# A shift row multiplied in native fp32 from the unsplit weights, in four column groups of the array

## The reference, cut to what matters

```
mod = c_act @ w_mod[l] + b_mod[l]
shift1, scale1, gate1, shift2, scale2, gate2 = split(mod, 6)
u = _rms(h, norm1_w[l]) * (1.0 + scale1) + shift1
proj = u @ w_in[l]                      # q, k, v, gates ... of the second block
...
u = _rms(h, norm2_w[l]) * (1.0 + scale2) + shift2
ff = silu(u @ w_gate[l]) * (u @ w_up[l])
h = h + gate2 * (ff @ w_down[l])
```

## Time and profile before

| | |
|---|---|
| median of 3 runs | 2783.16 us (2783.07 to 2783.49) |
| the profiled execution, its own time | 2784.83 us |
| its span, first to last instruction | 2783.0 us |
| PE busy | 2757.1 us (99%) |
| DVE, ACT, POOL busy | 2069.1, 1473.6, 335.8 us |
| mean granted TensorE clock | 0.998 of 2.4 GHz |
| share of the DMA engines' time | 66.7% |

### The profile page before, as it was taken

How to read it: one execution, slowest core, us unless ns; L and a number is a source line. 1 busy time by engine, 2 the same in 40 slices (tenths; PEclk the granted TensorE clock), 3 DMA queues, 4 the chain that set the end, 5 groups by cost and what they waited for, 6 DMA issues and landing times. The chain is left out here.

```text
span 2783.0 us, 43554 instructions
## 1 busy us (share of the span) xinstructions
PE 2757.1 (99%) x16354; PEld 2386.3 (86%) x16354; DVE 2069.1 (74%) x3601; ACT 1473.6 (53%) x2417; POOL 335.8 (12%) x1005
## 2 busy tenths in 40 slices
PE   7999999999999999999999999999999999999999
PEld 4778888888888888888888888888888888888888
DVE  3478877878988878787887777778888765566654
ACT  3365444545666676666667544545454443444443
POOL 0023300000002424224242310000000000000000
PEclk9999999999999999999999999999999999999999
DMA  8966668888965555555555588788768756655554
GB/s 325 352 226 212 205 204 271 286 270 294 303 177 194 175 175 174 173 181 166 182 178 172 177 278 280 258 285 296 263 209 287 247 183 188 197 189 186 189 183 148
DMA packets 183412, 621.87 MB, mean 223 GB/s; under 512 B 20241, under 2 KB 28705, under 8 KB 182433
## 3 DMA queue, kind: packets, MB, share of 16 engines
q1 hardware_dynamic: 183200, 619.09, 66.7%
HBM read 612.70 MB, written 4.21 MB: 222 GB/s over the span
## 5 line engine op out<-in xcount | busy, mean ns | idle before, releaser
L272 PE MATMUL ps<-act,whi 128*128 128x512 f32 (+1 forms) x6560 | 1763.6, 398 | 4.9 <-DVE act L257 3.0
L257 DVE TENSOR_TENSOR wlo<-raw,whi 128x1024 fp32r<-128x1024 f32 (+3 forms) x883 | 1045.3, 1189 | 437.0 <-ACT whi L248 244.1
L272 PEld LDWEIGHTS ps<-act,whi 128*128 128x128 f32 (+1 forms) x6560 | 1165.3, 189 | 217.3 <-issue 16.4
L272 PE MATMUL ps<-act,wlo 128*128 128x256 f32 (+2 forms) x6416 | 994.1, 287 | 0.4 <-DVE wlo L257 0.4
L248 ACT ACTIVATE whi<-raw 128x1024 fp32r<-128x1024 f32 (+3 forms) x883 | 880.2, 1024 | 175.8 <-PE ps L272 145.5
L272 PEld LDWEIGHTS ps<-act,wlo 128*128 128x128 f32 (+1 forms) x6416 | 896.7, 190 | 66.7 <-issue 1.7
L248 ACT ACTIVATE t<-ps 128x256 f32<-128x256 f32 (+2 forms) x420 | 157.3, 376 | 473.5 <-PE ps L272 445.6
L267 DVE SCALAR_TENSOR_TENSOR acc<-raw,c_act,acc 128x1024 f32<-128x1024 f32 x210 | 267.9, 1278 | 1.0 <-DMA raw<-in_w_mod 1.0
L248 ACT ACTIVATE t<-t 128x256 f32<-128x256 f32 (+3 forms) x258 | 114.5, 445 | 184.7 <-DVE t L257 152.0
L263 POOL TENSOR_SCALAR small<-small 128x2 f32<-128x2 f32 (+3 forms) x256 | 88.3, 345 | 972.8 <-DVE small L263 953.4
L257 POOL TENSOR_TENSOR small<-small 128x2 f32<-128x2 f32 (+2 forms) x460 | 160.0, 348 | 277.9 <-ACT t L248 187.3
(11 more groups left out here) (218 smaller groups left out, 1859.4 us busy)
## 6 DMA issues: line engine op xcount, KB each, us to landing
raw<-in_w SPq DMA_DIRECT2D x418, 512.0 KB, 4.9
raw<-in_w_mod SPq DMA_DIRECT2D x192, 512.0 KB, 4.6
raw<-in_w_gate SPq DMA_DIRECT2D x88, 512.0 KB, 4.6
raw<-in_w_up SPq DMA_DIRECT2D x88, 512.0 KB, 4.5
raw<-in_w_s SPq DMA_DIRECT2D x64, 512.0 KB, 6.8
raw<-in_w_out SPq DMA_DIRECT2D x64, 512.0 KB, 5.7
raw<-in_w_down SPq DMA_DIRECT2D x64, 448.0 KB, 3.7
raw<-in_w_ada SPq DMA_DIRECT2D x32, 512.0 KB, 5.1
```

What stands on the lines that cost most here:

```text
L257: return (q or DV).put(lambda e: e.tensor_tensor(o, a, b, op), needs, cost=max(0.4, size(o) * 0.0036) if q else 0.07 + size(o) * 0.00104)
L272: return PE.put(lambda e: e.matmul(o, w, x, start=start, stop=stop), needs, tell, cost)
```

## The change

`mm_shift` is called once per late block, ahead of the block's tile products. It multiplies the unsplit weights, straight from the `raw` slot, with the shift: four matmuls (one for each K tile of the block), 32 columns wide on the side of the shift, of which only the first is not zero, and 256 columns (two weight columns of 128) long, in native fp32. Each of the four goes to its own 32-row part of one PSUM bank. After late block 3 the bank's 256 columns are copied to SBUF by DVE, two matmuls against `C_SEL` add the four parts and turn the row into columns, and DVE copies the two sums. The shift no longer needs to be split: a tile of `t2` is filled with zeros by two ACT copies and its first column of each K tile with the shift by a third. The slot of a late piece is now free only when PE has read it too (`raw_free`).

```
--- before.py
+++ after.py
@@ -178,8 +178,6 @@
     at += 576
     SM = [place(f"small{i}", [128, 8], F32, at + 32 * i) for i in range(32)]
     at += 1024
-    SH = place("shift", [128, 16, 2], F32R, at)
-    at += 128
     T2 = [place(f"t2_{i}", [128, 512], F32, at + 2048 * i) for i in range(6)]
     T2R = [place(f"t2r_{i}", [128, 512], F32R, at + 2048 * i) for i in range(6)]
     T2R += [place(f"tx2r_{i}", [128, 512], F32R, a_c + 2048 * i) for i in range(4)]
@@ -471,7 +469,8 @@
             t = copy(hi, raw, it["in"] + (pe_free["hi", n - NH] if n >= NH else []))
             u = lo_part(lo, raw, hi, it["in"] + t + (pe_free["lo", n - NL] if n >= NL else []))
             it["hi"], it["lo"] = t, u
-            raw_free[it["raw"]] = t + u
+            if "late" not in it:
+                raw_free[it["raw"]] = t + u
         elif kind == "M":
             kt, half = it["kt"], it["half"]
             raw = RAW[it["raw"] % NR][:, 0:1024]
@@ -560,6 +559,8 @@
         hi, lo = HI[n % NH], LO[n % NL]
         last = None
         at = 0
+        if "late" in it:
+            mm_shift(it)
         for u in it["units"]:
             if it["kts"][0] == 0:
                 u.bank, free = grab_bank()
@@ -568,8 +569,6 @@
                 x, needs = ready(u.rhs, kt)
                 w = slice(at, at + 128)
                 mm_hi(u, hi[:, w], x, kt == 0, needs + it["hi"])
-                if "late" in it:
-                    mm_shift(it["late"], it["units"].index(u), kt, hi[:, w], lo[:, w], it["lo"])
                 last = mm_lo(u, lo[:, w], x, kt == 15, it["lo"], kt == it["kts"][-1])
                 at += 128
                 if kt != it["kts"][-1]:
@@ -581,27 +580,43 @@
         if "late" in it:
             for kt in it["kts"]:
                 state["used", it["late"], kt] = last
-            if kt == 15:
-                start(shift_sums(it["late"], last))
-
-    def mm_shift(name, i, kt, hi, lo, needs):
-
-        if kt == 0 and i == 0:
+
+    def mm_shift(it):
+
+
+        name, kts = it["late"], it["kts"]
+        if kts[0] == 0:
             while ("shift", name) not in state:
                 rest()
             state["sums", name], free = grab_bank()
-            PE.wait(free + state["shift", name])
-        o = state["sums", name][:, 2 * i:2 * i + 2]
-        mm(o, hi, SH[:, kt, :], kt == 0 and i == 0, False, cost=0.06)
-        mm(o, lo, SH[:, kt, :], False, kt == 15 and i == 1, needs, cost=0.06)
+            PE.wait(free + state["shift", name][1])
+        bank = state["sums", name]
+        tile = state["shift", name][0]
+        sh = tile[:, :].rearrange("p (k s) -> p k s", k=16)
+        w = RAW[it["raw"] % NR][:, :].rearrange("p (u k c) -> p u k c", u=2, k=4)
+        PE.wait(it["in"])
+        for k, kt in enumerate(kts):
+            last = mm(both(bank[32 * k:32 * k + 32, 0:256]), sh[:, kt, :], w[:, :, k, :], kt < 4, kt >= 12, tell=k == 3, cost=0.11)
+        raw_free[it["raw"]] = it["hi"] + it["lo"] + last
+        if kts[-1] == 15:
+            t2.give(tile, last)
+            start(shift_sums(name, last))
 
     def shift_sums(name, tok):
-        sm, f = yield from small.take()
-        yield from hop(tok + f)
+        rows, f = yield from t1.take()
+        sm, f2 = yield from small.take()
+        yield from hop(tok + f + f2)
         bank = state["sums", name]
-        k = copy_v(sm[:, 0:4], bank[:, 0:4], tok + f)
+        k = copy_v(rows[:, :], bank[:, 0:256], tok + f)
+        yield k
+        PE.wait(k)
+        for i in range(2):
+            t = mm(bank[:, 2 * i:2 * i + 2], rows[:, 128 * i:128 * i + 128], col(C_SEL, 2), True, True, tell=i == 1)
+        t1.give(rows, t)
+        yield from hop(t)
+        k = copy_v(sm[:, 4:6], bank[:, 0:4:2], t + f2)
         banks.give(bank, k)
-        state["offset", name] = sm, tt(sm[:, 4:6], sm[:, 0:4:2], sm[:, 1:4:2], ALU.add, k)
+        state["offset", name] = sm, k
 
     def join_late(name, i, bank, tok):
 
@@ -1184,7 +1199,7 @@
         state["halves", slot] = state.get(("halves", slot), 0) + 1
         if state["halves", slot] == 2:
             yield state["sec", slot]
-            section(slot, state["sec", slot])
+            yield from section(slot, state["sec", slot])
 
     def section(slot, needs):
 
@@ -1195,9 +1210,12 @@
         elif slot == M_MOD + 4:
             state["scale", "u2"] = stt(MOD[:, M_A2, :], MOD[:, slot, :], 1.0, col(C_N2, 16), ALU.add, ALU.mult, needs)
         elif slot in (M_MOD, M_MOD + 3):
-            h = copy(SH[:, :, 0], MOD[:, slot, :], needs + state.get(("used", "u", 15), []))
-            l = lo_part(SH[:, :, 1], MOD[:, slot, :], SH[:, :, 0], h)
-            state["shift", "u" if slot == M_MOD else "u2"] = h + l
+            tile, f = yield from t2.take()
+            yield from hop(needs + f)
+            sh = tile[:, :].rearrange("p (k s) -> p k s", k=16)
+            for i in range(2):
+                h = copy(sh[:, 8 * i:8 * i + 8, :], K1[:, 0:256].rearrange("p (k s) -> p k s", k=8), needs + f, scale=0.0)
+            state["shift", "u" if slot == M_MOD else "u2"] = tile, copy(sh[:, :, 0], MOD[:, slot, :], h)
 
     def m_items():
         secs = [(M_GATE, 0, C_BADA + 32, lambda kt, h: src["w_ada"][128 * kt:128 * kt + 128, 1024 * h:1024 + 1024 * h])]
```

## The result

The changed kernel takes 2795.41 us (median of 5 runs, 2793.02 to 2796.54), the kernel before 2783.27 (2783.07 to 2783.75). The ratio is 1.0040, 95% interval [1.0029, 1.0051]: the change makes the kernel about 12 us slower, where 2787.4 us and at most 2791 were forecast. The profiled execution took 2794.49 us.

What follows compares the result with a forecast made beforehand. PE's stream was taken as the bound, busy 2757.1 of 2783.0 us. Products -7.2, D1 stall +8.4, "u2" stalls +1.35 and clock +1.7 gave +4.2 on 2783.16: 2787.4 us, range 2778 to 2791 us.

Steps and rivals of the forecast that it cites:

- 6.9 us and half a piece: SP's queue, group "u": last constant issued at 794.5, landing at 801.9 us, between 801.3 and 802.7; ACT's slack was 2.2 us.
- PE's late blocks: Group "u": 3.55 us per late block, late block 3 from 791.8 to 795.4 us; late blocks of 16 instead of 20.
- SP's wait for PE: SP in group "u": DMA of D3's piece, ahead of S3's, waits for PE's shift product of late block 3, until 792.6 us.
- the L of K tile 4 and then of K tile 6 behind two `wlo`: DVE at D1: L 4 ready at 805.4, wanted at 801.4; L 6 at 810.0, behind the `wlo` of D2 and S2.
- products, both groups, with the selection: PE, both groups: 7.1 us go per group and 3.5 come, net 3.6 us per group, -7.2 us for both.
- stall of D1: PE in group "u": +8.4 us, 4.0 from the constants and 4.4 from two `wlo` ahead of L 6; bounds 2.0 and 9.2.
- lower clock: PE after the stalls: one stretch of 3.4 us of work at half pace loses 1.7 us; bounds 0 and 3.4.
- stalls of "u2": Group "u2": L of K tile 3 late by 1.05 us and K tile 11 by 0.3, +1.35 us; bounds 0 and 2.5.
- 0.76 us per visit: PE, late blocks: four new matmuls cost 0.76 us per visit, four visits per group, 3.0 us; bounds 0.57 and 1.1.
- Rival D: PE's late blocks: visits cost 1.1 instead of 0.76 us through changes of form, 2.7 us more; called improbable, no numeric chance.
- Rival A: Group "u": constants come in time, only DVE's order stalls D1, by 2.0 us; 2779.3 us in all; chance 0.20.
- rival C: D1: pauses leave PE at 1.2 GHz for 6.0 us of work or more; over 2788.7, up to 2791.1 us; chance 0.13.

Runs made afterwards that it cites:

- same_order: Changed kernel with only the three constant loads issued earlier on SP, planner still told the old times, so PE, ACT and DVE keep their orders: 2784.02 us.
- act_copies_late: Changed kernel, loads unmoved on SP, but the four ACT instructions behind the constants moved behind S3; the planner reordered DVE and PE too: 2781.34 us.
- held_slots: Kernel before with its own shift products, but late blocks' raw slots held until PE has done the block's first tile product: 2795.03 us.
- consts_early: Changed kernel with the three constant loads issued behind late block 0's piece, the planner told when they really come: 2778.35 us.
- early_cost19: consts_early with the planner told 0.19 instead of 0.11 us for each shift matmul: 2777.89 us, and 2777.60 us when run again.
- only_u2: The change made in group "u2" alone, group "u" as in the kernel before: 2781.82 us.
- small_first: Changed kernel with only the two 8 KB loads (ea, dtb) issued behind late block 0's piece, k staying behind the waiting pieces: 2794.58 us.

## Why the forecast was wrong

**The mechanism was right, two of its sizes were not.** Two steps failed. The last constant was to land 6.9 us and half a piece after its issue, and took 10.4 us. And the order of the second block was put at nothing, and cost 2.8 us.

PE's late blocks, SP's wait for PE, the constants behind it, ACT's queue, the L of K tile 4 and then of K tile 6 behind two `wlo`: each stands in the trace where the forecast has it, and same_order, act_copies_late and held_slots take it apart. The sign of the sum was forecast too, but not the size, and the forecast gave 0.57 to a time within 0.2% of before and only 0.28 to a slower one. Term by term, in us:

| term | forecast | measured | from |
|---|---|---|---|
| products, both groups, with the selection | -7.2 | -7.3 | twice 15.86 against 19.97 with the selection, 0.36 + 0.08 |
| stall of D1 | +8.4 | +11.0 | 7.99 + 3.02 |
| lower clock | +1.7 | +2.6 | half of 8.29 - 3.02 |
| stalls of "u2" | +1.35 | +2.2 | 1.12 + 1.07 |
| order of the second block | not there | +2.8 | 788.92 against 786.10 |
| sum | +4.2 | +11.3 | the medians differ by 12.1 |

**The products.** 0.76 us per visit and 0.4 for the selection were good to 0.1 us: late block 2 lasts 3.60 us in the trace, from 787.10 to 790.70, and eight tile products at 0.35 us leave 0.8 for the visit. Rival D, with 1.1, is out.

**The stall.** The mis-sized step is the landing of the last constant: 6.9 us and half a piece, at most 802.7 us, was taken over from a time when D3's piece stood 3.6 us ahead of S3's. Now the two were issued 0.5 us apart, right ahead of k. The forecast charged 1.35 us for a piece in the way, its bytes at the full 389 GB/s, and half of that; in the trace S3's piece took 3.1 us longer to land than before. The last packet of k came 2.8 us behind that instead of 1.7. Together with 0.2 us at the last count, and less the 0.8 us by which the last small load was issued later behind k, these are the 3.5 us between 6.9 and 10.4. The rate meanwhile was far below 389 GB/s:

```profile
795.00:803.00 8.00, 5.31 (x33) 4.42 (x31) 0.00 (x0) 0.00 (x0) 0.00 (x0) 1.00 0.93 274
```

The DMA engines were busy 93% of this stretch at 274 GB/s; no run shows why the rate was lower than in rows 12. The rest of the difference is that the group began 1.16 us earlier in this execution, so that D1 was due at 800.15 instead of 801.4. Against that, the second part was 3.0 instead of 4.4 us, because PE at half clock took longer to reach K tile 6.

Rival A's price of 2.0 us is what same_order measured, 1.7 + 0.3; its chance of 0.20 was high for a slack of 2.2 us against an issue moved by more than 5 us.

The sentence on the page "DMA: Bandwidth & Descriptors" of the Trainium skill (anatomy of one DMA), about 2.0 us and the bytes at 436 GB/s, is a fit to single DMAs issued from GpSimd. It gives an estimate of 4.0 us for k, where k's last packet ended after 7.1 us before, and after 11.2 us now. Here SyncE issued, and no transfer was alone; no run tells which of the two matters.

**The clock.** It fell while PE stood still and came back at 816.4, after 5.3 us of work at the lower pace instead of the 3.4 taken from the row near the start. That is inside the bounds, and rival C's mechanism in part; rival C had asked for 6.0 us or more. The 0.8 us by the Trainium skill ("TensorE: Matmul & The Clock Gate", the section on how the oscillation bites in real kernels) were a third of it.

**What was left out altogether.** The forecast compared the orders only around the two groups; its sum has no term for what comes later. The planner writes the rest of the program from its own clock, and that clock had moved: 13 more batches of small products and 1.6 us of small waits over the second block. same_order has them without the stall of 8 us; consts_early, early_cost19 and only_u2 (362, 361 and 361 batches, 786.0, 786.3 and 786.1 us) don't have them. With the measured sizes of the first four terms and without this one, the sum is +8.5, or 2791.7 us, 0.7 above the range, so the late landing, with the clock behind it, reaches just past the range, and this term carries the time well out of it.

**What stays open.** The reason that a batch more costs about 0.2 us (2.8 / 13) was not measured by itself; held_slots (4.3 us for 15 batches, 3.4 of them idle) shows that waits and batches come mixed. Of the 12.1 us of the medians, 0.8 are not accounted for; runs of the changed kernel differ by up to 3.5 us. (The spans of the two traces differ by only 9.7 us, of which the 1.16 us by which group "u" began earlier is a part: 11.3 - 1.16 = 10.1.)

## What to carry to other kernels

A buffer that is freed by a later reader delays everything that stands behind its refill on the issuing queue, and what is hurt may be on a third engine: look at what follows on the queue of the DMAs first, and move the transfers that wait for nothing ahead of those that do. Take the time to landing from a stretch with as many bytes issued right ahead as there will be, and price a transfer in the way by such a stretch too, not by the fullest rate. Where several loads count up one semaphore, only the last landing in the profile is to be trusted. Where a planner writes the order, compare the whole program, and tell the planner the cost that was measured.

## What the hardware showed unexpectedly

- Two matmuls of 2 columns cost 0.22 us in a stream of long ones: 0.57 against 0.35 us per tile product; the late blocks gave 4.1 us back for 64 of them less four visits.
- The issue of the last 8 KB load held SP for 2.39 us in the changed kernel and for 1.30 before. That the DMA engines are busy is not the whole reason: in small_first they were busy 84% of the time from 755 to 757 us, and there the two small issues, without k ahead of them, took 0.46 and 0.42 us. In same_order, at the same place but right behind k, the second took 2.24 us.
- Loads that share a semaphore hide each other's landing: the profile's 7.5 us for k was the 16th of 48 counts, at 799.84, while k's last packet ended at 803.59. The forecast of small_first rested on the first of these numbers, and failed.
